# Sorting experts by token count, and six more weight slots, in a two-layer hybrid trunk with a mixture of experts

## The chip, the cores and the metric

The kernel runs on one core of one Trainium2 chip. The metric is the device time of one execution in microseconds; of several runs the median is given.

## The reference

A trunk of two layers runs over 256 tokens at once: 128 context tokens and 128 latent tokens, each of 1024 values. A layer modulates and normalises the tokens, projects them, runs three branches (differential attention, a long convolution, a retention), merges them and adds the result. Then comes a grouped mixture of experts (MoE), the part that the change touches. All arithmetic is in float32.

```python
def moe(h, w_router, b_router, w1, w3, w2):
    scores = jax.nn.softmax((h @ w_router).astype(jnp.float32), axis=-1)
    sel = scores + b_router.astype(jnp.float32)
    grp = sel.reshape(sel.shape[:-1] + (N_GROUPS, EXP_PER_GROUP))
    gscore = lax.top_k(grp, TOP_K)[0].sum(-1)
    gidx = jnp.argmax(gscore, axis=-1)
    ...
    _, eidx = lax.top_k(masked, TOP_K)
    ...
    a = jnp.einsum('bld,edf->blef', h, w1)
    b = jnp.einsum('bld,edf->blef', h, w3)
    act = jax.nn.silu(a) * b * gate[..., None].astype(h.dtype)
    return jnp.einsum('blef,efd->bld', act, w2)
```

There are 16 experts, each token goes to two of them, and an expert has w1 and w3 of 1024x512 and w2 of 512x1024. So 512 places are taken in a layer, 32 for an expert on average.

## The kernel before, in words

**The stream of weights.** All weights are cut into pieces of 128x2048 float32 (1.05 MB). `PLAN` lists every group of pieces in the order in which SyncE's queue fetches them; `ring_table` gives each piece its slot in `ring`, which has 8 slots. Piece n is fetched once n - 7 pieces have been consumed (`s_weights_used`). A dense unit (an input projection, an output projection, half a merge branch) takes one piece, a modulation (`ada`) four, and the MoE of a layer 102. TensorE consumes the pieces in the same order. The MoE fetch is line 534, that of the single item lines 526 and 539, that of dense pieces line 512.

**The MoE.** After the output projection (line 922) the router picks two experts for each token; a modulation `ada(layer, 5)` (line 637) and small matmuls lie between. An expert's tokens are then numbered, and `picks` on VectorE builds a matrix of zeros and ones that gathers them. Eight items follow of two experts each, `PAIRS` of them, with 64 places for an expert. An item p on TensorE is: `moe_in` (line 1014), four blocks, in each of which two experts' matmuls stream 256 columns through two tiles of 64 stationary columns side by side; `gather` of item p + 1 (lines 987 and 997); `act_turn` (line 1039), which transposes the activations; `moe_out` of item p - 1 (line 1050), two halves of 512 columns; and `combine` (line 1092), which adds the scaled result to every token in PSUM banks 0 to 3. ScalarE and VectorE copy and activate between these steps.

A ninth item, the single, has one expert of at most 64 further places, chosen on chip: the first block by which an expert passes 64 places. Its weights are fetched once more. If there are more such blocks, each engine branches to `more_block`, which fetches and computes them one after the other. The single's matmuls are lines 1029, 1069 and 1079.

In layer 0 the items 4 to 7 also carry the filter of the next layer (`filter_step`).

**Other queues.** GpSimd's queue loads parameters and the caches `kc`, `vc` and `sc` of the next layer (line 573 on), exchanges halves for the rotary, stores the new cache entries (lines 587 and 590), and broadcasts rows for the router. The branch buffers (`qk`, `mix`, `kc`, `vc`, `sc`, `filt`, `ysp`, `attr`, `qx`, `xi`, `probs`, `amix`, `amixT`) are tensors of their own, and nothing uses most of them during the MoE.

Of the kernel before, what the change touches and what calls it, by code (L numbers as in the profile page):

```python
# [38 lines left out]
PAIRS = N_EXPERTS // 2  # L39
BLOCK = 64  # L40

MORE = 2 * TOK // (BLOCK + 1) - 1
OVER = (TOK - 1) // BLOCK
# [8 lines left out]
SLOTS = 8  # L52

# [7 lines left out]
ITEMS = PAIRS + 1  # L61
MOE_PIECES = 6 * N_EXPERTS + 6
# [45 lines left out]
def ring_table():  # L108

    pieces = [(item, c) for item in PLAN for c in range(PLAN_PIECES[item[0]])]  # L110
    done = [(item, c) for item in DONE for c in range(PLAN_PIECES[item[0]])]
    slot, count, filled = [], [], [0] * SLOTS
    for n, piece in enumerate(pieces):
# [4 lines left out]
    return slot, count  # L118

SLOT, FILL = ring_table()
# [23 lines left out]
def ff_end(layer, p):  # L145

    before = END["moe", layer, 0] - MOE_PIECES
    return before + 8 * min(p + 1, PAIRS) + 4 * (p // PAIRS) + 4 * max(p - 1, 0)

def y_end(layer, p, half):
# [3 lines left out]
    return ff_end(layer, p + 1) + 2 * (half + 1)  # L155
# [92 lines left out]
def trunk_program(nc, row_scratch, weights, experts, mod_params, params, consts, shared, x_in, k_cache, v_cache, s_cache,  # L248
                  y_out, k_out, v_out, s_out):
    with ExitStack() as ctx:  # L250
# [20 lines left out]
        s_extra_known = sem("extra_known")  # L271
# [92 lines left out]
        s_weights_in = [sem(f"weights_in{slot}") for slot in range(SLOTS)]  # L364
# [20 lines left out]

        ring = sb("ring", P, SLOTS, PIECE)
        cst = sb("cst", P, N_CST)
# [6 lines left out]
        qk = sb("qk", P, 8, TOK)  # L394
        mix = sb("mix", P, 8, TOK)
# [4 lines left out]
        kc = sb("kc", P, H_A, SEQ)  # L400
        vc = sb("vc", P, H_A * DV_A)
        sc = sb("sc", P, H_C, 2, DV_C)
        filt = sb("filt", P, 3, C_B)
        zt = sb("zt", P, C_B)
        ysp = sb("ysp", P, 2, C_B)
        tmp = sb("tmp", P, C_B)
        attr = sb("attr", P, H_C, SEQ)
        qx = sb("qx", P, 2, 2, SEQ)
        dsum = sb("dsum", P, H_C, SEQ)
        xi = sb("xi", P, 2, 2, SEQ)  # L410
        probs = sb("probs", P, 2, 2, 2 * SEQ)
        amix = sb("amix", P, 2, 2 * SEQ)
        amixT = sb("amixT", P, 2, 2 * SEQ)
# [15 lines left out]
        ints = ctx.enter_context(nc.sbuf_tensor("ints", [P, 3], mybir.dt.int32))  # L429
# [3 lines left out]
        xsel = sb("xsel", P, 8)  # L433
# [15 lines left out]
        rows_sb = amixT[0:16, 0, 0:P]  # L449
# [53 lines left out]
        def _(sp):  # L503
            sp.dma_start(x[:, :, :], x_in).then_inc(s_x_in, 16)
            sp.dma_start(shd[:, :], shared).then_inc(s_shared_in, 16)
            n = dense = 0
            for kind, layer, _ in PLAN:
                for _ in range(0 if kind == "moe" else PLAN_PIECES[kind]):
                    if n >= SLOTS:

                        sp.wait_ge(s_weights_used, n - SLOTS + 1)
                    sp.dma_start(ring[:, SLOT[n], :], weights[dense, :, :]).then_inc(
                        s_weights_in[SLOT[n]], 16)
                    n += 1
                    dense += 1
                if kind != "moe":
                    continue
                for p in range(PAIRS + 1):
                    todo = [(2 * p + c % 2, c // 2) for c in range(8)] if p < PAIRS else []
                    if p == PAIRS:  # L520

                        sp.wait_ge(s_extra_known, layer + 1)
                        e = sp.value_load(ints[0:1, 2:3], min_val=0, max_val=N_EXPERTS - 1)
                        for part in (0, 2, 1, 3):
                            sp.wait_ge(s_weights_used, n - SLOTS + 1)
                            sp.dma_start(ring[:, SLOT[n], :], experts[layer, bass.ds(e, 1), part, :, :]
                                         .rearrange("a p c -> (a p) c")).then_inc(
                                             s_weights_in[SLOT[n]], 16)
                            n += 1
                    todo += [(2 * p - 2 + c % 2, 4 + c // 2) for c in range(4)] if p else []  # L530
                    for e_, part in todo:

                        sp.wait_ge(s_weights_used, n - SLOTS + 1)
                        sp.dma_start(ring[:, SLOT[n], :], experts[layer, e_, part]).then_inc(
                            s_weights_in[SLOT[n]], 16)
                        n += 1
                for part in (4, 5):
                    sp.wait_ge(s_weights_used, n - SLOTS + 1)
                    sp.dma_start(ring[:, SLOT[n], :], experts[layer, bass.ds(e, 1), part, :, :]
                                 .rearrange("a p c -> (a p) c")).then_inc(s_weights_in[SLOT[n]], 16)  # L540
                    n += 1
# [7 lines left out]
        def _(pool):  # L549
# [15 lines left out]
            for layer in range(DEPTH):  # L565
# [38 lines left out]
        def _(pe):  # L604
# [10 lines left out]
            def piece(width):  # L615
# [4 lines left out]
                return ring[:, SLOT[n], :].rearrange("p (k n) -> p k n", n=width)  # L620
# [381 lines left out]
            def moe_in(layer, p):  # L1002
# [3 lines left out]
                pe.wait_ge(s_hgat_hi, ITEMS * layer + p + 1)  # L1006
                for half in range(2):
# [1366 lines left out]
```

## Time and profile before

| what | value |
|---|---|
| median of 3 runs (lowest to highest) | 1264.77 us (1264.11 to 1270.05) |
| the profiled execution, its span | 1267.2 us |
| TensorE matmuls, busy | 1228.1 us (97%) |
| TensorE weight loads, busy | 929.2 us (73%) |
| VectorE, ScalarE, busy | 363.3 and 222.0 us |
| bytes moved | 362.06 MB, mean 286 GB/s |
| fetches of expert pieces | 204, of 1024 KB |
| fetches of dense pieces | 128, of 1024 KB |

The profiled execution is one of its own, beside the three timed runs. Its time is the span, from the first to the last instruction. A busy TensorE is one that has a matmul in its pipeline, not one at its peak. In the trace a float32 matmul stands as two instructions, each of which streams all its columns.

### The profile page before, as it was taken

What the parts mean: (1) busy time and instruction counts of PE and PEld (TensorE: products, weight loads), DVE (VectorE), ACT (ScalarE), POOL (GpSimd) and SP (SyncE); (2) the same over time, 40 slices, a digit from 0 to 9 for tenths busy, and PEclk for the clock granted to TensorE, in tenths of its full rate; (3) what the DMA queues carried; (4) which work ended last, traced back from release to release, by engine and by line L of the source; (5) the groups of instructions that cost most, each with busy time, mean ns of one, the idle gap of its engine ahead of it and who ended that gap; (6) DMA issues with size and microseconds to landing.
All of it is one profiled execution on the core that took longest, in us unless ns stands there. A gap on an engine that the chain in (4) does not pass through costs nothing.

```text
span 1267.2 us, 18560 instructions
## 1 busy us (share of the span) xinstructions
PE 1228.1 (97%) x7762; PEld 929.2 (73%) x7762; DVE 363.3 (29%) x917; ACT 222.0 (18%) x469; POOL 39.5 (3%) x80
## 2 busy tenths in 40 slices
PE   6999999999999999999999999999999999999996
PEld 5678888888897666666558888887888776666663
DVE  2441153134236111111233223423243611111113
ACT  2141013231030100111124101223202010000011
POOL 1001110000000000000000012000000000000000
PEclk9899999999989999999999999999999999999999
DMA  9779443424967999999976844343345599999992
GB/s 387 315 290 388 140 158 127 147 100 151 350 254 313 417 421 421 420 420 420 418 293 253 361 161 143 129 141 134 122 149 195 236 418 421 421 420 420 420 421 111
DMA packets 52601, 362.06 MB, mean 286 GB/s; under 512 B 6592, under 2 KB 6752, under 8 KB 9760
## 3 DMA queue, kind: packets, MB, share of 16 engines
q1 hardware_dynamic: 48672, 350.33, 69.3%
q0 software_dynamic: 3840, 10.47, 2.4%
q8 instruction: 64, 1.05, 0.3%
q14 instruction: 25, 0.20, 0.0%
HBM read 356.56 MB, written 2.64 MB: 283 GB/s over the span
## 4 chain that ended last, share of the span: by engine, by line
PE 86%; DMA 9%; DVE 2%; ACT 1%; issue 1%; SPq 0%; DVEq 0%; ACTq 0%
PE bank L713 24%; PE bank L1014 13%; PE bank L1050 9%; DMA ring<-in_experts 7%; PE bank L893 7%; PE bank L997 5%; PE bank L922 4%; PE bank L708 4%; PE bank L637 4%; PE bank L1092 3%; DMA ring<-in_weights 2%; PE bank L724 2%; PE bank L1029 1%; PE bank L973 1%; PE bank L697 1%
## 5 line engine op out<-in xcount | busy, mean ns | idle before, releaser
L713 PE MATMUL bank<-h,ring 128*128 128x256 f32 x1472 | 326.3, 380 | 0.0
L713 PEld LDWEIGHTS bank<-h,ring 128*128 128x128 f32 x1472 | 276.8, 190 | 40.9 <-issue 4.4
L1014 PE MATMUL bank<-ring,gates 128*64 128x256 f32 x2048 | 226.2, 380 | 8.0 <-DMA ring<-in_experts 4.3
L1014 PEld LDWEIGHTS bank<-ring,gates 128*64 128x64 f32 x2048 | 152.1, 137 | 79.7 <-issue 11.6
L1050 PE MATMUL bank<-ring,gates 128*64 128x512 f32 x512 | 113.4, 595 | 0.0
L1050 PEld LDWEIGHTS bank<-ring,gates 128*64 128x64 f32 x512 | 35.3, 137 | 66.7 <-issue 66.7
L997 PE MATMUL bank<-uc,gates 128*128 128x128 f32 x576 | 67.9, 276 | 0.1
L997 PEld LDWEIGHTS bank<-uc,gates 128*128 128x128 f32 x576 | 65.9, 192 | 0.7 <-DVE uc L1612 0.4
L1616 DVE SCALAR_TENSOR_TENSOR gates<-gates,bank 128x512 f32<-128x512 f32 (+1 forms) x18 | 11.8, 658 | 172.6 <-issue 161.3
L1092 PEld LDWEIGHTS bank<-gates,uc 128*128 128x128 f32 x256 | 47.3, 190 | 18.8 <-issue 13.0
L1092 PE MATMUL bank<-gates,uc 128*128 128x256 f32 x256 | 59.5, 386 | 0.0
L708 PE MATMUL bank<-ring,h 128*128 128x256 f32 x256 | 56.4, 379 | 0.0
L922 PE MATMUL bank<-uc,ring 128*128 128x256 f32 x256 | 55.6, 379 | 0.0
L922 PEld LDWEIGHTS bank<-uc,ring 128*128 128x128 f32 x256 | 48.6, 190 | 6.6
L708 PEld LDWEIGHTS bank<-ring,h 128*128 128x128 f32 x256 | 48.1, 190 | 6.2
L1556 ACT ACTIVATE gates<-bank 128x512 f32<-128x512 f32 (+1 forms) x18 | 10.3, 574 | 240.6 <-PE bank L1014 218.7
L637 PE MATMUL bank<-ring,condT 128*32 128x256 f32 x768 | 46.6, 397 | 3.9 <-DMA ring<-in_weights 3.2
L2115 DVE COPY uc<-bank 128x512 f32<-128x512 f32 x16 | 11.1, 692 | 134.9 <-PE bank L1050 134.9
L724 PE MATMUL bank<-h,ring 128*128 128x256 f32 x192 | 43.2, 382 | 2.5 <-ACT h L1268 2.5
L724 PEld LDWEIGHTS bank<-h,ring 128*128 128x128 f32 x192 | 36.0, 190 | 9.4 <-issue 4.6
L637 PEld LDWEIGHTS bank<-ring,condT 128*32 128x32 f32 x768 | 25.8, 114 | 22.5 <-issue 9.7
L1423 ACT ACTIVATE gates<-bank,sm 128x256 f32<-128x256 f32 x48 | 20.1, 471 | 104.9 <-PE bank L713 104.9
(258 smaller groups left out, 1077.6 us busy)
## 6 DMA issues: line engine op xcount, KB each, us to landing
ring<-in_experts SPq DMA_DIRECT2D x204, 1024.0 KB, 11.7
ring<-in_weights SPq DMA_DIRECT2D x128, 1024.0 KB, 6.5
cst<-in_consts POOLq DMA_DIRECT2D x1, 1345.0 KB, 11.2
x<-in_x_in SPq DMA_DIRECT2D x1, 1024.0 KB, 5.0
sc<-in_s_cache POOLq DMA_DIRECT2D x2, 512.0 KB, 10.0
probs<-qk POOLq DMA_DIRECT2D x32, 32.0 KB, 3.0
va<-row_scratch POOLq DMA_DIRECT2D x2, 512.0 KB, 7.2
vr<-row_scratch POOLq DMA_DIRECT2D x2, 512.0 KB, 9.2
```

Source lines behind the costliest of these rows:

```text
L637: last = pe.matmul(bank[b][32 * j:32 * j + 32, 0:256], condT[:, k, :], w[j][:, k, :], start=(k == 0), stop=(k == KT - 1), skip_group_check ...
L697: last = pe.matmul(bank[4][:, 0:TOK], ones[:, :], h[:, k, :], start=(k == 0), stop=(k == KT - 1))
L708: last = pe.matmul(bank[b][:, g * 256:(g + 1) * 256], h[:, k, g_cols(g)], w[:, k, :], start=(k == 0), stop=(k == KT - 1))
L713: last = pe.matmul(bank[b][:, c * TOK:(c + 1) * TOK], w[:, k, c * P:(c + 1) * P], h[:, k, :], start=(k == 0), stop=(k == KT - 1))
L724: last = pe.matmul(bank[u][:, c * TOK:(c + 1) * TOK], w[:, k, c * P:(c + 1) * P], h[:, k, :], start=(k == 0 and c == 0), stop=(k == KT - 1 ...
L893: last = pe.matmul(bank[b][:, c * TOK:(c + 1) * TOK], w[:, k, d * P:(d + 1) * P], src[:, k, :], start=(k == 0), stop=(k == 3))
L922: last = pe.matmul(out[c], w[:, k, c * P:(c + 1) * P], merged[:, k, :], start=(k == 0), stop=(k == KT - 1))
L997: last = pe.matmul(bank[4 + half][:, c * P:(c + 1) * P], htok[:, g, k * P:(k + 1) * P], pick[p % 2][:, g, :], start=(g == 0), stop=(g == 1))
L1014: last = pe.matmul(bank[b][64 * j:64 * j + 64, half * 256:half * 256 + 256], hgat[:, k, 64 * j:64 * j + 64], w[j][:, k, :], start=(k == 0) ...
L1050: last = pe.matmul(bank[5 - half][64 * j:64 * j + 64, :], actT[p % 2][:, f, 64 * j:64 * j + 64], w[j][:, f, :], start=(f == 0), stop=(f == ...
L1092: last = pe.matmul(bank[dt // 2][:, (dt % 2) * TOK:(dt % 2 + 1) * TOK], ysb[:, dt * P:(dt + 1) * P], matrix, start=(fresh and dt % 2 == 0) ...
L1423: last = sc_e.activation(gates[:, t, :], src[:, c, :], ACT.Tanh, scale=0.5, bias=b_half[:, t:t + 1])
```

## The change

The largest and the smallest experts get items of their own kinds. `ITEM_KINDS` replaces the eight pairs and a single with five pairs, a `wide` item (one expert, 128 places), a `quad` item (four experts, 32 places each, in four tiles of 32 columns) and a `single`, which now is one expert fetched once, with its two halves side by side. Experts 12 to 15 are fixed in the first two pairs. Experts 0 to 11 are sorted by their count of tokens on VectorE (`sort`), and fetched by the expert number that the sort leaves in `ints`: the largest is the wide item, the four smallest the quad. No expert is fetched twice, so a layer's MoE takes 96 pieces. `further` counts blocks that don't fit their room; they go to `more_block` as before.

Six further slots are lent to the ring during the MoE. The tensor `lent` has six slots of 2048 columns, in which the branch buffers now lie; only MoE pieces use them, once the last merge piece is consumed and the stores are done. The loads of `kc`, `vc` and `sc` for layer 1 wait for the end of the MoE of layer 0.

```diff
+ITEM_KINDS = ("pair", "pair", "wide", "quad", "pair", "pair", "pair", "single")
+ITEMS = len(ITEM_KINDS)
+PAIRS = ITEMS - 1
+SORTED = 12
+ITEM_EXPERTS = ((12, 13), (14, 15), (0,), (8, 9, 10, 11), (1, 2), (3, 4), (5, 6), (7,))
+FIXED_ITEMS = 2
+WIDE_ROOM, SMALL_ROOM = 128, 32
-MORE = 2 * TOK // (BLOCK + 1) - 1
-OVER = (TOK - 1) // BLOCK
+MORE = 2 * TOK // (BLOCK + 1)
+OVER = (TOK - 1 - SMALL_ROOM) // BLOCK + 1
 SLOTS = 8
+LENT = 6
-MOE_PIECES = 6 * N_EXPERTS + 6
+MOE_PIECES = 6 * N_EXPERTS
...
-        at = n if n < SLOTS else slot[pieces.index(done[n - SLOTS])]
+        lent = range(SLOTS, SLOTS + LENT) if kind == "moe" else ()
+        since = {at: free[at] for at in range(SLOTS)}
+        since.update({at: max(free[at], END["merge", layer, 5]) for at in lent})
+        at = min(since, key=lambda n: (since[n], n))
...
+                sp.wait_ge(s_stores_read, layer + 1)
...
+                for p in range(ITEMS):
+                    if p == FIXED_ITEMS:
+                        sp.wait_ge(s_order_known, layer + 1)
+                    many = len(ITEM_EXPERTS[p])
...
+                    for part in (0, 2, 1, 3) if ITEM_KINDS[p] == "single" else range(4):
+                        for j in range(many):
+                            fetch(expert(p, j, part))
...
+                else:
+                    pool.wait_ge(s_weights_used, END["moe", layer - 1, 0])
                 pool.dma_start(kc[:, :, :], k_cache[layer]).then_inc(s_cache_in, 16)
...
-                        w = piece(256), piece(256)
+                        w = [piece(256) for _ in range(many)]
                         for k in range(KT):
-                            for j in range(2):
-                                last = pe.matmul(bank[b][64 * j:64 * j + 64, half * 256:half * 256 + 256],
-                                                 hgat[:, k, 64 * j:64 * j + 64], w[j][:, k, :],
+                            for j in range(many):
+                                rows = slice(width * j, width * j + width)
+                                last = pe.matmul(bank[b][rows, half * 256:half * 256 + 256],
+                                                 hgat[:, k, rows], w[j][:, k, :],
...
-                    if layer + 1 < DEPTH and p >= 4:
-                        filter_step(layer + 1, p - 4)
+                    if layer + 1 < DEPTH and p >= 3:
+                        filter_step(layer + 1, p - 3)
...
+                def sort():
+                    key, at = place[:, 0, :], place[:, 1, :]
+                    first = C("xf")[:, 0:SORTED]
...
+                    link(stt(key, count[:, 0:SORTED], float(N_EXPERTS), first, ALU.mult, ALU.subtract))
+                    link(tt(square, across(key), down(key), ALU.is_gt))
+                    link(dve.tensor_reduce(at, square, AX.X, ALU.add))
+                    link(stt(places_of[:, :, :], across(at), 1.0, down(first), ALU.add, ALU.is_equal))
+                    link(tt(square, places_of[:, :, :], across(first), ALU.mult))
+                    link(dve.tensor_reduce(key, square, AX.X, ALU.add))
+                    ts(ints[:, 2:2 + SORTED], key, -1.0, ALU.add, 0.0, ALU.max).then_inc(s_order_known, 1)
...
                 gathered(0)
+                sort()
...
                     if p == 0:
-                        block_of(1, ints[:, 2:3], xsel[:, 0:2], xsel[:, 2:4])
-                        dve.sem_inc(s_extra_known, 1)
+                        sort_tokens(sorted_rank, rank)
+                        sort_tokens(sorted_gate, gate)
                         mod_add(layer, 5, 1)
+                        rooms()
+                        further()
```

`sort_tokens` multiplies ranks (or shares) by the matrix of places and adds over experts, two operations of 288 elements; `rooms` writes each expert's room in five; `further` is the former count of blocks (three comparisons, now four after a subtraction, then a running sum in 12 operations), moved from ahead of the first item into it. `picks` builds two operations for each tile and group of tokens, so 4 in the wide item, 8 in a pair and 16 in the quad.

## Rows read from the trace of the kernel before

**Rows 1.** The page: GB/s moved in 40 slices of the span.
```profile
GB/s 387 315 290 388 140 158 127 147 100 151 350 254 313 417 421 421 420 420 420 418 293 253 361 161 143 129 141 134 122 149 195 236 418 421 421 420 420 420 421 111
```
**Rows 2.** The chain of waits, by line, share of the span.
```profile
by line: PE bank L713 24.2%; PE bank L1014 12.8%; PE bank L1050 8.9%; DMA ring<-in_experts 6.8%; PE bank L893 6.6%; PE bank L997 5.2%; PE bank L922 4.4%; PE bank L708 4.4%; PE bank L637 3.6%; PE bank L1092 2.9%; DMA ring<-in_weights 2.5%; P
```
**Rows 3.** Timeline of TensorE, one pair item: start us, us, instructions.
```profile
470.97 14.03 PE L1014 MATMUL bank<-ring,gates 128*64 128x256 f32 x128
...
485.21 3.74 PE L997 MATMUL bank<-uc,gates 128*128 128x128 f32 x32
...
489.31 7.09 PE L1050 MATMUL bank<-ring,gates 128*64 128x512 f32 x32
496.33 3.72 PE L1092 MATMUL bank<-gates,uc 128*128 128x256 f32 x16
499.98 14.25 PE L1014 MATMUL bank<-ring,gates 128*64 128x256 f32 x128
```
**Rows 4.** Timeline of TensorE, input blocks that waited (in brackets) for a fetch.
```profile
540.37 3.67 PE L1014 MATMUL bank<-ring,gates 128*64 128x256 f32 x32 [0.23 <-DMA ring<-in_experts]
...
571.33 3.67 PE L1014 MATMUL bank<-ring,gates 128*64 128x256 f32 x32 [1.29 <-DMA ring<-in_experts]
...
1118.58 3.67 PE L1014 MATMUL bank<-ring,gates 128*64 128x256 f32 x32 [0.36 <-DMA ring<-in_experts]
...
1208.66 3.67 PE L1014 MATMUL bank<-ring,gates 128*64 128x256 f32 x32 [0.62 <-DMA ring<-in_experts]
```
**Rows 5.** Timeline of TensorE, first and last matmuls of the two MoE stages.
```profile
393.15 14.03 PE L1014 MATMUL bank<-ring,gates 128*64 128x256 f32 x128 [0.69 <-ACT gates L1536]
...
645.76 2.94 PE L1079 MATMUL bank<-gates,uc 64*128 64x256 f32 x16 [0.79 <-ACT uc L1547]
...
1000.81 14.03 PE L1014 MATMUL bank<-ring,gates 128*64 128x256 f32 x128 [0.69 <-ACT gates L1536]
...
1250.44 2.94 PE L1079 MATMUL bank<-gates,uc 64*128 64x256 f32 x16 [0.79 <-ACT uc L1547]
```
**Rows 6.** Stretches of time: busy us by engine, PEclk, DMA share, GB/s.
```profile
360.00:365.00 5.00, 5.00 (x25) 4.41 (x24) 1.34 (x5) 0.84 (x3) 0.00 (x0) 1.00 0.36 87
...
380.00:385.00 5.00, 5.00 (x76) 3.39 (x74) 3.93 (x15) 0.00 (x0) 0.00 (x0) 0.93 0.02 7
```
**Rows 7.** Groups by line: busy us, mean ns of one, idle before.
```profile
L713 PE MATMUL bank<-h,ring 128*128 128x256 f32 x1472 | 326.3, 380 | 0.0
...
L1014 PE MATMUL bank<-ring,gates 128*64 128x256 f32 x2048 | 226.2, 380 | 8.0 <-DMA ring<-in_experts 4.3 <-ACT gates L1536 3.7
...
L1050 PE MATMUL bank<-ring,gates 128*64 128x512 f32 x512 | 113.4, 595 | 0.0
...
L637 PE MATMUL bank<-ring,condT 128*32 128x256 f32 x768 | 46.6, 397 | 3.9 <-DMA ring<-in_weights 3.2 <-DVEq L1622 0.7
...
L1608 DVE TENSOR_TENSOR dsum<-dsum,zt 128x256 f32<-128x256 f32 x14 | 5.9, 422 | 1.5
```
**Rows 8.** Issue to landing of line 534's fetches; timeline of GpSimd, stores.
```profile
DMA to landing us min/median/max: 4.7/11.6/16.8
...
207.35 1.08 POOL L590 DMA_DIRECT2D s_out<-mix  x2 [25.97 <-ACT mix L1455]
```
**Rows 9.** TensorE's modulation after a pause, the clock there, and without one.
```profile
40.66 6.35 PE L637 MATMUL bank<-ring,condT 128*32 128x256 f32 x64 [2.91 <-DMA ring<-in_weights]
...
40.00:50.00 10.00, 9.34 (x79) 5.97 (x80) 0.63 (x4) 1.44 (x2) 0.00 (x0) 0.69 0.24 86
...
381.54 3.66 PE L637 MATMUL bank<-ring,condT 128*32 128x256 f32 x64
```
**Rows 10.** Timeline of VectorE, the first MoE item of layer 0.
```profile
398.26 0.21 DVE L1616 SCALAR_TENSOR_TENSOR tmp<-cnt 128x48 f32<-128x48 f32 x1
...
404.40 0.69 DVE L1616 SCALAR_TENSOR_TENSOR gates<-gates,bank 128x512 f32<-128x512 f32 x1 [2.15 <-ACT gates L1556]
```

More of the change, by code:

```diff
@@ L111, in ring_table @@
     done = [(item, c) for item in DONE for c in range(PLAN_PIECES[item[0]])]
-    slot, count, filled = [], [], [0] * SLOTS
-    for n, piece in enumerate(pieces):
-        at = n if n < SLOTS else slot[pieces.index(done[n - SLOTS])]
+    gone = {piece: n + 1 for n, piece in enumerate(done)}
+    free, filled = [0] * (SLOTS + LENT), [0] * (SLOTS + LENT)
+    slot, count, used = [], [], []
+    for (kind, layer, _), c in pieces:
+        lent = range(SLOTS, SLOTS + LENT) if kind == "moe" else ()
+        since = {at: free[at] for at in range(SLOTS)}
+        since.update({at: max(free[at], END["merge", layer, 5]) for at in lent})
+        at = min(since, key=lambda n: (since[n], n))
         filled[at] += 1
@@ L117, in ring_table @@
         count.append(filled[at])
-    return slot, count
-SLOT, FILL = ring_table()
+        used.append(since[at])
+        free[at] = gone[(kind, layer, _), c]
+    return slot, count, used
+SLOT, FILL, USED = ring_table()
 ADA_ORDER = [item[1:] for item in PLAN if item[0] == "ada"]
@@ L147, in ff_end @@
     before = END["moe", layer, 0] - MOE_PIECES
[L148 removed]
+    return before + sum(ITEM_IN[:p + 1]) + sum(ITEM_OUT[:max(p - 1, 0)])
 def y_end(layer, p, half):
@@ L154, in y_end @@
         return END["moe", layer, 0]
-    return ff_end(layer, p + 1) + 2 * (half + 1)
+    return ff_end(layer, p + 1) + ITEM_OUT[p] // 2 * (half + 1)
 def combined(layer, p):
@@ L363, in trunk_program @@
         s_vr_copied = sem("vr_copied")
-        s_weights_in = [sem(f"weights_in{slot}") for slot in range(SLOTS)]
+        s_weights_in = [sem(f"weights_in{slot}") for slot in range(SLOTS + LENT)]
         s_weights_used = sem("weights_used")
@@ L393, in trunk_program, with part @@
         uc = sb("uc", P, 12, TOK)
-        qk = sb("qk", P, 8, TOK)
-        mix = sb("mix", P, 8, TOK)
+        def part(slot, at, n):
+            return lent[:, slot, at:at + n]
+        qk = part(0, 0, 2048).rearrange("p (a b) -> p a b", a=8)
+        mix = part(1, 0, 2048).rearrange("p (a b) -> p a b", a=8)
         qkr = mix[:, 0:4, :]
@@ L506, in _, with fetch @@
             n = dense = 0
-            for kind, layer, _ in PLAN:
[L508 to L515, printed above, removed]
+            def fetch(source):
+                nonlocal n
+                if USED[n]:
+                    sp.wait_ge(s_weights_used, USED[n])
+                slot = ring[:, SLOT[n], :] if SLOT[n] < SLOTS else lent[:, SLOT[n] - SLOTS, :]
+                sp.dma_start(slot, source).then_inc(s_weights_in[SLOT[n]], 16)
+                n += 1
@@ L516, in _ @@
+            for kind, layer, _ in PLAN:
                 if kind != "moe":
+                    for _ in range(PLAN_PIECES[kind]):
+                        fetch(weights[dense, :, :])
+                        dense += 1
                     continue
[L518 to L536, printed above, removed]
@@ L537, in _ @@
                 for part in (4, 5):
[L538 to L541, printed above, removed]
+                    fetch(expert(PAIRS, 0, part))
             for c in range(4):
@@ L2144, in _, with further @@
-                upto = src
-                ts(ints[:, 0:1], upto[:, OVER * N_EXPERTS - 1:], -1.0, ALU.add, 0.0,
-                   ALU.max).then_inc(s_more_known, 1)
+                def further():
+                    nonlocal upto, other
+                    beyond = place[:, :, :].rearrange("p a b -> p (a b)")[:, 0:N_EXPERTS]
+                    link(tt(beyond, count, room[:, :], ALU.subtract))
+                    for c in range(OVER):
+                        link(ts(flags[:, 16 * c:16 * c + 16], beyond, float(BLOCK * c), ALU.is_gt))
+                    src, dst = flags, upto
+                    step = 1
+                    while step < OVER * N_EXPERTS:
+                        link(dve.tensor_copy(dst[:, 0:step], src[:, 0:step]))
+                        link(tt(dst[:, step:], src[:, step:], src[:, :OVER * N_EXPERTS - step], ALU.add))
+                        src, dst = dst, (other if dst is upto else upto)
+                        step *= 2
+                    upto = src
+                    dve.tensor_copy(ints[:, 0:1], upto[:, OVER * N_EXPERTS - 1:]).then_inc(s_more_known, 1)
@@ L2164, in block_of @@
-                    link(ts(red[:, 1:2], red[:, 1:2], -float(BLOCK), ALU.mult))
+                    level = one.rearrange("p (c e) -> p e c", e=N_EXPERTS)
+                    byexp, start, part_ = tmp[:, 64:80], tmp[:, 80:96], tmp[:, 96:112]
+                    link(dve.tensor_reduce(byexp, level, AX.X, ALU.add))
+                    link(tt(part_, byexp, C("xf")[:, 0:16], ALU.mult))
+                    link(dve.tensor_reduce(red[:, 0:1], part_, AX.X, ALU.add))
+                    link(ts(expert, red[:, 0:1], -1.0, ALU.add, 0.0, ALU.max))
@@ L2165, in block_of @@
+                    link(tt(start, byexp, room[:, :], ALU.mult))
+                    for c in range(1, OVER):
+                        link(stt(start, one[:, 16 * c:16 * c + 16], float(BLOCK * c), start, ALU.mult, ALU.add))
+                    link(dve.tensor_reduce(red[:, 1:2], start, AX.X, ALU.add))
+                    link(ts(red[:, 1:2], red[:, 1:2], -1.0, ALU.mult))
                     wide_ = tmp[:, 128:160].rearrange("p (a b) -> p a b", a=2)
```

170 lines of the change are left out of this document (96 added, 74 removed).

## The prediction

> **What bounds the kernel now.** I read the row of bytes moved over the span first [rows 1]: twice, for about eight and about seven slices of 31.7 us, transfers run flat at 420 GB/s, and these are the two mixture-of-experts (MoE) stages. Outside them they run at 120 to 350. The chain of waits [rows 2] puts 6.8% on the expert fetches and most of the rest on TensorE, so neither limit stands alone. The timeline of one pair item [rows 3] shows why: TensorE goes from one item's first matmul (470.97) to the next one's (499.98) in 29.01 us without a pause: input matmuls 14.0, gathers and turns 4.4, output matmuls 7.0, combine 3.65. A pair needs 12 pieces of weights of 1.05 MB. Where TensorE does wait for a fetch in layer 1, the first and last such waits end 90.1 us apart [rows 4] with 36 pieces between: 2.50 us a piece, 30.0 us a pair. So an item costs 29.0 on TensorE and 30.0 on the DMA engines, and the eight-slot lead hides the difference: the six waits of both layers add up to 4.3 us [rows 4, 7], 1.5 of it in layer 0. The MoE stages last 393.15 to 648.70 and 1000.81 to 1253.38 [rows 5], 255.6 and 252.6 us; layer 0 is longer by the filter matmuls of layer 1.
>
> Ahead of a stage the ring is full and the transfers idle: 87 GB/s in 360 to 365, 7 GB/s in 380 to 385 [rows 6]. That is the room that lent slots could fill.
>
> **Part 1: one item fewer.** Before there are eight pairs and a single; after, seven full-length items and a single. I take TensorE's time for each form. The wide item has one expert over all 128 columns: 16 passes of 128x256 per block at 326.3/1472 = 0.222 us, 3.55 us a block as against 14.03/4 = 3.51 for a pair [rows 3, 7]; it fetches 6 pieces. The quad has four 32-column tiles side by side and fetches 24. Four-way tiles of 256 columns are in the trace, in the modulation (line 637): 64 instructions in 3.66 us [rows 9], the size of one quad block, so 3.6 us where a pair takes 3.51. Four-way with 512 columns (quad output) is not in the trace; nearest is line 1050, two-way at 113.4/512 = 0.221 a pass [rows 7]. If four run at once it is 0.11 each, 7.1 us per item as for a pair; if only two at once, 14.2. Line 637 has four at once at 46.6/768 = 0.061, so I take 7.1. Not less, since the same columns stream. The whole item therefore disappears: 29.0 us of TensorE time per layer.
>
> **Part 2: 96 pieces for 102.** The expert with over 64 places was fetched a second time. Six pieces of 2.50 are 15.0 us of transfer per layer.
>
> **Part 3: six lent slots.** Slots 8 to 13 come free when the last merge piece is consumed, before the output projection. There are then 14 pieces in flight or landed when the first item starts, not 8. The idle room of [rows 6] takes the six: the transfers are far from busy in the 25 us before 385. The last four of the 14 wait, as four do now, for the modulation that ends at 385.2 [rows 9]. Six pieces by 2.50 are another 15.0 us of lead per layer. The fetch queue also waits for the stores of the branch outputs; the last is issued at 207.35 [rows 8], over 130 us earlier, so nothing.
>
> **What is then late: the transfers at the quad.** TensorE alone would gain 29.0 + 1.5 and 29.0 + 2.8, but the quad asks for 24 pieces in 29 us and the fetch gives 11.6. I walked the stage piece by piece: a piece lands 2.50 us after the one before it, or, if its slot was released late, 4.7 us after the release (the shortest issue-to-landing of these fetches [rows 8]). Layer 0: pieces 11 to 14 are released at 385.2 and land to 397.4. Every piece up to 43 arrives before TensorE wants it; around the wide item, which frees 6 slots in its 29 us, all 14 are full and the transfers pause 8 us in all. At the quad's first block (471.2) number 40 lands and 32 are wanted; its fourth block wants number 44 at 482.0, just as it lands, a wait of 0.1. Pair 4 is served. The quad's second output half wants number 62 at 523.1 and it lands at 527: a wait of 4.0. Then 0.5 and 1.5 in pair 5's last two blocks, and none after: the last items want fewer pieces than arrive (number 96 at 612, wanted at 617.4). In all 6.1 us: the stage ends at 393.15 + 225.4 + 6.1 = 624.7 as against 648.7, **24.0 less** (225.4 is 255.6 - 1.5 - 29.0, plus 0.4 for the slightly longer quad blocks). Layer 1 lacks the filter matmuls, so the same walk has waits of 4.4, 0.8, 1.5 and 0.9 with the 0.1, 7.7 in all: 252.6 - 2.8 - 29.0 + 0.4 + 7.7 = 228.9 us, **23.7 less**.
>
> **The clock behind such a wait.** A pause of 2.91 us before line 637 at 40.66 is followed by 6.35 us for 64 instructions that take 3.66 elsewhere, and the granted clock of 40 to 50 is 0.69: part of it ran at the lower level of 1.2 GHz [rows 9]. The wait of 4.0 is longer, so I add 2.7 per layer. Half or more is absorbed, since the waits that follow (1.9 in layer 0, 3.2 in layer 1) are for pieces that don't come later for it: 0.8 and 0. The Trainium skill, "TensorE: Matmul & The Clock Gate", HAM oscillation, says that waits for a transfer between bursts of matmuls drop the clock, each time anew; the trace agrees with its one pause. By that rule the sum is as here; without it 0.8 less.
>
> **The small steps.** VectorE's sort (7 operations, at most 144 elements), sorting of ranks and shares (4, of 288), room (5) and two more operations in the count of further blocks come in; the block search (15 operations) goes from the first item. At 0.21 for 48 elements and 0.42 for 256 [rows 7, 10] that is 2.5 + 1.8 + 1.0 + 0.4 - 3.4 = 2.3 us more, ahead of an operation before which VectorE now idles 2.15 [rows 10]. The activation's second operation waits for TensorE as long again. I cost it at 0; above, if every operation cost 0.42, some 4 us more would be late and go to TensorE's turn of the first item, 2 to 4 per layer. Below, no gain: the path was not VectorE's. The order is known near 394, while piece 21, the first that needs it, has its slot released at 407. The fetch queue's reading of an expert number is in the trace too (the single), and an issue costs it 0.34 us per 2.50. Quad picks are 16 operations for 8, some 1.5 us more under 14 us of input matmuls. The caches of layer 1 are loaded after the MoE of layer 0 instead of in its idle room: 1 MB, 2.5 us, in GpSimd's queue, wanted some 17 units of 7.1 us (32 passes of 0.222) later, and the next thing in that queue waits for unit 7 anyhow: 0. Filter steps only move an item forward.
>
> **Sum.** 24.0 + 23.7 - 0.8 = 46.9 us. The profiled execution's span is 1267.2, 2.4 above the median of the runs; off the median 1264.8 it is **1217.9 us**, span about 1220.
>
> **Rivals.**
> *TensorE alone decides (12%).* If pieces land a little earlier than in my walk or TensorE is held elsewhere anyway, the waits vanish: 2 x 29.0 + 4.3 = 62.3, 1202.5 us; with a third of the waits 1207. For it: the measured waits are as small as 0.2. Against: 24 pieces in 29 us cannot come from the stream.
> *The lent slots bring little (12%).* If their fetches start late or crowd out other transfers, each missing slot costs 2.50 per layer, first at the quad's input; all six: 30.0, so 1248. Half: 1233. Against: the idle rows.
> *Quad tiles overlap only in pairs (6%).* Input and output of the quad each double, 21 us per layer, of which about 8 hide in the waits: 1244. Line 637 speaks against it for the input.
> *An expert does not fit its room (slower, 3%).* The wide item serves only the largest of experts 0 to 11, and 12 to 15 keep 64 places. No instruction of the further-block branch is in the trace, so now at most one expert per layer passes 64, once. Routing the reference's own inputs gives expert 2, with 85 and 91; next come 43 and 50, and the fourth smallest of the first twelve has 27 and 15 for 32 places. If instead an expert of 12 to 15 passed 64, or the fourth smallest 32, a serial block runs: six fetches through two buffers, about 4.1 us each ((3.55 + 4.7)/2), gather, activations and combine, some 40 us. In both layers that is 1218 + 80 = 1298; it decides against the change from two such blocks.
> *My forecast (64%)* spans 1208 to 1230; the remaining 3% is for outcomes that none of these names, two thirds of it no change.
>
> **How the numbers follow.** The range takes the forecast's own, three quarters of the first rival and two thirds of the second: 1204 to 1240. About 0.5% (6 us) is what a measurement of this kernel can tell. Slower is the last rival, 0.03; within 0.5%, 0.02; the rest faster, 0.95.
>
> **What would show it.** MoE stages of 231 and 229 us; 96 expert fetches per layer, 192 in all; no or one short gap in transfers until the quad; TensorE's longest wait for a fetch, 4 us, before the second half of the quad's output, followed by slowed matmuls; quad blocks of 3.6 us. Wrong if the quad's blocks take 7 us, if large waits stand in the quad's input (a lead that did not form), or if rows of the further-block branch appear.

## The result

The changed kernel took 1218.28 us (median of 4 runs, 1217.30 to 1220.16) where the kernel before took 1265.04 (4 runs): a ratio of 0.962, 95% interval 0.959 to 0.965, 46.8 us less. The forecast was 1217.9. The profiled execution was the slowest of the four: its span is 1218.4 and its own time 1220.16, so 1.8 us lie around the span.

The page of the changed kernel, its rates in 40 slices, answers to [rows 1]. A slice is now 30.5 us.

```profile
PEclk8999999999998999999999999999999899999998
DMA  9879534333797998999986945343247599899992
GB/s 383 339 284 393 183 130 142 136 112 139 278 408 306 405 401 341 421 421 420 421 331 258 373 153 165 113 147 138 107 155 314 231 391 416 326 423 420 421 420 109
```

Two things are to be seen. The idle room ahead of the MoE is used: the two slices that end near 366 us carry 278 and 408 where two slices at about that place carried 350 and 254, and the same 5 us that moved 87 GB/s before [rows 6] now move 423:

```profile
360.00:365.00 5.00, 5.00 (x25) 4.40 (x24) 1.98 (x6) 2.00 (x6) 0.00 (x0) 1.00 1.01 423
380.00:385.00 5.00, 4.50 (x74) 2.86 (x66) 2.23 (x6) 0.38 (x1) 0.00 (x0) 1.00 0.12 16
```

From 380 to 385 the transfers are idle as before: all slots that are free are filled. And there is a dip inside each stage (341, 326) that the kernel before did not have: the ring is full there, around the wide item.

The issues of transfers on the same page, with KB each and the median from issue to landing:

```profile
ring<-in_weights SPq DMA_DIRECT2D x128, 1024.0 KB, 5.7
ring<-in_experts SPq DMA_DIRECT2D x108, 1024.0 KB, 20.9
lent<-in_experts SPq DMA_DIRECT2D x84, 1024.0 KB, 16.7
```

108 and 84 are 192 expert pieces, where there were 204. They are under way for 17 to 21 us instead of 12, because more are queued.

The timeline of TensorE in layer 0 (start, length, instructions, in brackets the idle time before) from the first to the last matmuls of the stage answers to [rows 3 to 5]:

```profile
391.40 10.58 PE L1056 MATMUL bank<-lent,gates 128*64 128x256 f32 x96 [0.69 <-ACT gates L1580]
...
440.12 13.98 PE L1056 MATMUL bank<-ring,gates 128*128 128x256 f32 x64
...
468.92 3.86 PE L1056 MATMUL bank<-lent,gates 128*32 128x256 f32 x66
...
480.86 0.41 PE L1056 MATMUL bank<-ring,gates 128*32 128x256 f32 x2 [1.37 <-DMA lent<-in_experts]
...
488.74 7.03 PE L1095 MATMUL bank<-lent,gates 128*128 128x512 f32 x16
...
517.86 0.62 PE L1095 MATMUL bank<-ring,gates 128*32 128x512 f32 x2
...
526.36 5.13 PE L1095 MATMUL bank<-lent,gates 128*32 128x512 f32 x32 [4.86 <-DMA lent<-in_experts]
531.42 3.72 PE L1136 MATMUL bank<-gates,uc 128*128 128x256 f32 x16
...
620.60 2.94 PE L1123 MATMUL bank<-gates,uc 64*128 64x256 f32 x16 [0.79 <-ACT uc L1591]
```

The stage lasts 391.40 to 623.54, 232.1 us (before 255.6), and in layer 1, by the same rows, 975.29 to 1204.58, 229.3 us (before 252.6). The two stages together are 46.7 us shorter, which is all that the medians differ by. The first half of the quad's output starts at 517.86; its matmuls run until 521.5, then comes the longest wait of the stage. The granted clock of the 10 us around that wait is 0.83 (third number from the end):

```profile
520.00:530.00 10.00, 5.14 (x36) 1.29 (x32) 0.00 (x0) 1.88 (x2) 0.00 (x0) 0.83 1.01 420
```

TensorE's waits over the whole changed kernel (sum, times, longest):

```profile
PE bank L1095 <- DMA lent<-in_experts: 9.5, 2, 4.9
...
PE bank L1056 <- ACT gates L1580: 3.7, 4, 1.2
...
PE bank L1056 <- DMA lent<-in_experts: 3.5, 2, 2.1
...
PE bank L1056 <- DMA ring<-in_experts: 1.3, 3, 0.6
```

14.3 us of waits for expert fetches, where there were 4.3: the change adds waits, and still gains, because the item that went was worth more.

### The profile page after: what moved, and what is told of

The parts are those of the page before. It is cut to its first block, busy times and chain, and to the rows that moved or that the text cites. A ratio compares the mean times of both kernels' runs of the same rounds, so it can differ in the third digit from the quotient of the medians.

```text
span 1218.4 us, 18282 instructions
## 1 busy us (share of the span) xinstructions
PE 1171.0 (96%) x7494; PEld 897.5 (74%) x7494; DVE 359.9 (30%) x905; ACT 216.3 (18%) x459; POOL 39.5 (3%) x80
## 3 DMA queue, kind: packets, MB, share of 16 engines
q8 instruction: 62, 1.02, 0.3%
## 4 chain that ended last, share of the span: by engine, by line
PE 87%; DMA 8%; DVE 2%; ACT 1%; SPq 1%; issue 1%; DVEq 0%; ACTq 0%
PE bank L752 25%; PE bank L1056 12%; PE bank L1095 7%; PE bank L932 7%; PE bank L961 5%; PE bank L747 5%; PE bank L1036 4%; DMA ring<-in_experts 4%; PE bank L763 4%; PE bank L1136 4%; PE bank L676 4%; DMA lent<-in_experts 3%; DMA ring<-in_weights 1%; PE bank L1071 1%; PE bank L1012 1%; SPq L541 1%
## 5 line engine op out<-in xcount | busy, mean ns | idle before, releaser
L752 PEld LDWEIGHTS bank<-h,ring 128*128 128x128 f32 x1472 | 276.8, 190 | 40.9 <-issue 4.4
L1056 PE MATMUL bank<-ring,gates 128*64 128x256 f32 (+2 forms) x1280 | 148.7, 379 | 7.1 <-DMA lent<-in_experts 3.5
L1056 PEld LDWEIGHTS bank<-ring,gates 128*64 128x64 f32 (+2 forms) x1280 | 104.3, 137 | 45.4 <-issue 7.5
L1095 PE MATMUL bank<-lent,gates 128*64 128x512 f32 (+2 forms) x288 | 67.0, 637 | 9.5 <-DMA lent<-in_experts 9.5
L1056 PE MATMUL bank<-lent,gates 128*64 128x256 f32 (+1 forms) x640 | 64.7, 380 | 1.4 <-ACT gates L1580 1.4
L932 PE MATMUL bank<-lent,ring 128*128 128x256 f32 x256 | 56.4, 380 | 0.0
L1056 PEld LDWEIGHTS bank<-lent,gates 128*64 128x64 f32 (+1 forms) x640 | 39.2, 126 | 21.2 <-issue 2.3
L1095 PEld LDWEIGHTS bank<-lent,gates 128*64 128x64 f32 (+2 forms) x288 | 21.3, 141 | 44.9 <-issue 44.9
L932 PEld LDWEIGHTS bank<-lent,ring 128*128 128x128 f32 x256 | 48.4, 190 | 6.9 <-issue 0.4
L1136 PE MATMUL bank<-gates,uc 128*128 128x256 f32 x224 | 51.9, 385 | 0.0
```

The lines of the kernel that those rows point to most:

```text
L752: last = pe.matmul(bank[b][:, c * TOK:(c + 1) * TOK], w[:, k, c * P:(c + 1) * P], h[:, k, :], start=(k == 0), stop=(k == KT - 1))
L932: last = pe.matmul(bank[b][:, c * TOK:(c + 1) * TOK], w[:, k, d * P:(d + 1) * P], src[:, k, :], start=(k == 0), stop=(k == 3))
L1056: last = pe.matmul(bank[b][rows, half * 256:half * 256 + 256], hgat[:, k, rows], w[j][:, k, :], start=(k == 0), stop=(k == KT - 1), skip_g ...
L1095: last = pe.matmul(bank[5 - half][rows, :], actT[p % 2][:, f, rows], w[j][:, f, :], start=(f == 0), stop=(f == 3), skip_group_check=True)
L1136: last = pe.matmul(bank[dt // 2][:, (dt % 2) * TOK:(dt % 2 + 1) * TOK], ysb[:, dt * P:(dt + 1) * P], matrix, start=(fresh and dt % 2 == 0) ...
```

## The experiments

Each ran beside the kernel before on its chip; those of one group shared the chip and its runs. The length of a MoE stage is read from the timeline of the profiled execution as above. What lies outside the two stages took between 752.8 and 759.1 us in these profiled executions, whatever the variant, so a difference of a few us between two medians need not come from the MoE; the stages are the better measure. The profile of one_block is taken apart in its own paragraph.

| run | time, us | ratio to before, 95% interval | stages, layer 0 and 1, us |
|---|---|---|---|
| changed kernel | 1218.28 | 0.962 (0.959 to 0.965) | 232.1, 229.3 |
| no_lent | 1254.53 | 0.989 (0.986 to 0.992) | 251.5, 247.8 |
| lent_alone | 1258.32 | 0.993 (0.990 to 0.995) | 253.3, 248.9 |
| quad_first | 1215.58 | 0.957 (0.952 to 0.961) | 230.8, 226.8 |
| half_fetch | 1209.43 | 0.954 (0.951 to 0.957) | 233.2, 219.3 |
| after_again | 1217.22 | 0.961 (0.959 to 0.963) | 232.3, 229.7 |
| busy_wait | 1219.80 | 0.963 (0.961 to 0.964) | 232.2, 229.7 |
| quad_late | 1217.13 | 0.962 (0.960 to 0.964) | 231.7, 228.9 |
| quad_first_busy | 1210.05 | 0.955 (0.953 to 0.956) | 229.0, 225.3 |
| sort_four | 1219.26 | 0.963 (0.960 to 0.965) | 233.2, 229.8 |
| one_block | 1266.57 (one run) | | |

**no_lent: the new items, eight slots.**

```diff
-        lent = range(SLOTS, SLOTS + LENT) if kind == "moe" else ()
+        lent = ()
```

> The new items with a ring of 8 slots; nothing is lent. By the walk of the prediction the transfers are six pieces behind at the quad: six times 2.50 us in each layer, stages of 232 + 15 and 229 + 15 us, 1218 + 30 = 1248 us, with TensorE's waits in the quad's input blocks (about 1, 7 and 6 us). Rival: the lead is not what counts, since 96 pieces of 2.50 us fit into a stage anyway; then within 5 us of 1218.

1254.5, so the rival falls: the lead does count, and the six slots are worth 36 us beside the new items (38 by the stages). That is 6 more than walked. The quad's input blocks on the timeline of this run:

```profile
470.71 3.66 PE L1056 MATMUL bank<-ring,gates 128*32 128x256 f32 x64
476.35 5.35 PE L1056 MATMUL bank<-ring,gates 128*32 128x256 f32 x64 [1.98 <-DMA ring<-in_experts]
488.42 6.15 PE L1056 MATMUL bank<-ring,gates 128*32 128x256 f32 x64 [6.72 <-DMA ring<-in_experts]
498.34 6.31 PE L1056 MATMUL bank<-ring,gates 128*32 128x256 f32 x64 [3.77 <-DMA ring<-in_experts]
```

The waits are where the walk put them (2.0, 6.7, 3.8 for 1, 7, 6), and the quad's output waits 5.6 more. The blocks behind the three take 5.4 to 6.3 us instead of 3.7. Set against the changed kernel, layer 0 has 11.7 us more of waits, less than the walked 15, and 7.6 us of slower matmuls and restarts. The walk had no clock in it, and the clock is what was missing:

```profile
480.00:490.00 10.00, 3.28 (x48) 1.82 (x44) 0.00 (x0) 0.00 (x0) 0.00 (x0) 0.83 1.00 419
490.00:500.00 10.00, 6.23 (x68) 3.10 (x64) 0.69 (x1) 0.60 (x1) 0.00 (x0) 0.67 1.00 400
```

Granted clock (third from the end) 0.83 and 0.67, transfers busy all the time.

**lent_alone: the old items, fourteen slots.**

```diff
--- (the kernel before)
-        at = n if n < SLOTS else slot[pieces.index(done[n - SLOTS])]
+        lent = range(SLOTS, SLOTS + LENT) if kind == "moe" else ()
+        ...
+        at = min(since, key=lambda n: (since[n], n))
```

with the branch buffers moved into `lent` as in the change.

> The items of the kernel before (eight pairs, a single, 102 pieces) with the six lent slots. By the walk TensorE is then the only limit: the 4.3 us of waits go, 1265 - 4 = 1261 us. Rival: the lead is worth 15 us per layer by itself, as it is at the quad: 1235 us.

1258.3, 8.8 us under the kernel before on that chip. No wait for an expert fetch is left, and the stages are 2.3 and 3.6 us shorter, 5.9 in all: the 4.3 of waits and the 0.2 to 0.3 that each of the six had cost beyond its own length (in layer 0 an item with a wait of 0.23 took 29.82 us and takes 29.37 here). The rest lies outside the stages, where executions vary. The lead alone is worth little: TensorE has its 29 us an item.

The two parts by themselves gain 12.6 and 8.8 us, 21 together (8.9 and 5.9 in the stages); both at once gain 46.8 to 49.7 (46.7 in the stages). Fewer items without a lead run into the transfers, a lead without fewer items runs into TensorE.

**half_fetch: TensorE without a limit by transfers, in layer 1.** Part of the weights is missing from layer 1's MoE.

```diff
+                if half:
+                    slot, source = slot[:, 0:PIECE // 2], source[:, 0:PIECE // 2]
                 sp.dma_start(slot, source).then_inc(s_weights_in[SLOT[n]], 16)
...
-                            fetch(expert(p, j, part))
+                            fetch(expert(p, j, part), layer == 1)
```

> The changed kernel, but in layer 1 each expert piece is fetched only in its first half of columns, so that part of the weights is missing from layer 1's MoE. Transfers can't limit that stage. If the waits for fetches are the only thing between TensorE's own 221 us and the measured 229.3, the stage takes 221.2 us (252.6 - 2.8 - 29.0 + 0.4) and the kernel 1218 - 8 = 1210 us. Rival: other waits (copies, VectorE's longer first item) hold part of it: 224 us or more.

The stage of layer 1, which lasts until 1191.50:

```profile
972.25 10.58 PE L1058 MATMUL bank<-lent,gates 128*64 128x256 f32 x96 [0.69 <-ACT gates L1582]
...
1188.57 2.94 PE L1125 MATMUL bank<-gates,uc 64*128 64x256 f32 x16 [0.79 <-ACT uc L1593]
```

It takes 219.3 us: 10.0 less than in the changed kernel, 1.9 under the 221.2 walked. So neither copies nor VectorE hold the stage beyond the walk, as the rival had it, and the whole distance between TensorE's own time and the measured stage is 7.9 us of waits and 2.1 of slower matmuls and restarts behind them.

The 1.9 below the walk can be taken apart on the timelines. The waits of the kernel before had cost 0.9 more than their length, the 0.4 for slower quad blocks does not exist (a quad block takes 3.5 us, like a pair's), and the items around the wide one and the quad go 0.7 faster (28.92, 28.80 and 28.65 us from first matmul to first matmul, where a pair between pairs takes 29.01). Set against lent_alone, which has the old items and no waits either, the new items save 29.7 us in layer 1 (248.9 to 219.3), where 29.0 was forecast.

**quad_first: the quad third, the wide fourth.**

```diff
-ITEM_KINDS = ("pair", "pair", "wide", "quad", "pair", "pair", "pair", "single")
+ITEM_KINDS = ("pair", "pair", "quad", "wide", "pair", "pair", "pair", "single")
```

(and the experts' places in `ITEM_EXPERTS` likewise)

> The changed kernel with the quad as third item and the wide one as fourth. The walk gives waits of 1.1 (quad's input) and 0.2 and 1.5 in the item after next, none in the quad's output, since the wide item, which takes 6 pieces, follows at once: 3.7 us less in layer 0 and 4.9 in layer 1, and the 1.5 us of slowed matmuls behind the long wait go too, partly. 1218 - 9 = 1209 us, between 1207 and 1211. Rival: the order doesn't matter because the bytes are the same: 1218 us.

1215.6, with runs of 1207.9, 1214.0, 1217.1 and 1217.4: neither the forecast nor clearly the rival. The interval of its ratio (0.952 to 0.961) overlaps that of the changed kernel (0.959 to 0.965); the stages are 1.3 and 2.5 us shorter. In the profiled execution, the one of 1217.1, the wait in the quad's input was 4.95 us, not 1.1, and the block behind it ran at half the clock:

```profile
456.40 0.64 PE L1056 MATMUL bank<-lent,gates 128*32 128x256 f32 x2 [4.95 <-DMA ring<-in_experts]
```

```profile
450.00:455.00 5.00, 1.45 (x28) 0.62 (x20) 0.69 (x1) 0.60 (x1) 0.00 (x0) 0.88 1.02 423
455.00:460.00 5.00, 3.60 (x36) 2.02 (x40) 0.00 (x0) 0.00 (x0) 0.00 (x0) 0.50 1.01 421
```

The transfers never stopped (423 and 421 GB/s), so piece 36 came 3.9 us later than walked with the bytes on time. The last section says what was seen of it.

**quad_late: the quad sixth, the wide seventh.**

```diff
-ITEM_KINDS = ("pair", "pair", "wide", "quad", "pair", "pair", "pair", "single")
+ITEM_KINDS = ("pair", "pair", "pair", "pair", "pair", "quad", "wide", "single")
```

(and the experts' places likewise)

> The changed kernel with the quad as sixth and the wide as seventh item. The walk gives one wait, 3.8 us in the quad's input, and stages 3.0 and 3.9 us shorter than in the walk of the changed kernel; the late landings seen with the quad as third item (3.5 us later than walked) take some of it back, and a pause costs clock: between 1209 and 1216, 1212 us. Rival: the order doesn't matter beyond the noise: 1218 us.

1217.1 against 1217.2 of the unaltered kernel: no gain, just above the expected bound. The walk's one wait of 3.8 is 6.2 us in layer 0 and 6.6 in layer 1, with a slow block behind:

```profile
542.06 0.64 PE L1056 MATMUL bank<-ring,gates 128*32 128x256 f32 x2 [6.22 <-DMA lent<-in_experts]
```

The stages are 231.7 and 228.9 us where the walk gives 228.5 and 225.0.

**after_again and busy_wait: the clock behind the long wait.**

> The changed kernel unaltered, as the base for its variants on the same chip: 1218 us, between 1216 and 1221.

```diff
                 for half in range(2):
+                    if many == 4 and half:
+                        take(5 - half)
+                        for _ in range(18):
+                            pe.matmul(bank[5 - half][:, 0:P], ones[:, :], ones[:, :], start=True, stop=True)
...
                     w = [piece(512) for _ in range(many)]
```

> The changed kernel with 18 dummy matmuls (about 4.5 us, a third of whose time at most can stick out) issued ahead of the wait for the second half of the quad's output. If the matmuls behind the wait are slow (5.1 us for 3.6) because TensorE paused, they take 3.6 us now, and in layer 1, and less in layer 0, up to 1.5 us is gained: 1216.5 us, a difference near what can be measured; the trace row decides. Rival: they are slow because of the interleaved fetches or tiles: then still 5.1 us, and 1218 us or more.

The trace shows the mechanism without its gain:

```profile
518.77 4.29 PE L1093 MATMUL bank<-ones 128*128 128x128 f32 x36
...
523.61 3.64 PE L1100 MATMUL bank<-lent,gates 128*32 128x512 f32 x32 [0.55 <-DMA lent<-in_experts]
...
543.47 3.67 PE L1056 MATMUL bank<-ring,gates 128*64 128x256 f32 x32 [1.29 <-DMA ring<-in_experts]
```

The half behind the wait takes 3.64 us and not 5.13, so it was the pause. But the next item's fourth block now waits 1.29 for its fetch (0.16 in the changed kernel), and the stages are 232.2 and 229.7, as in the kernel without dummies (232.3 and 229.7 in after_again). The transfers set the pace until that block, and a slow TensorE costs nothing while they do. The median is no better either: 0.963 (0.961 to 0.964) against 0.961 (0.959 to 0.963).

**quad_first_busy: dummies in the order of quad_first.**

```diff
--- (quad_first)
+                        if many == 4 and (half, b) == (1, 7):
+                            for _ in range(12):
+                                pe.matmul(bank[7][:, 256:256 + P], ones[:, :], ones[:, :], start=True,
+                                          stop=True, skip_group_check=True)
                         w = [piece(256) for _ in range(many)]
```

> Quad as third item, with 12 dummy matmuls (about 3 us) ahead of the wait for the fourth block of its input. The four runs of that order without them spread from 1207.9 (granted clock 0.993) to 1217.4 us (0.984). If the spread is the clock behind the 5 us wait, it closes here near the fast end: 1209 to 1211 us with a clock of 0.99. Rival: the spread has another cause (transfers that land late by chance), the dummies change nothing: 1215 us, same spread.

1210.05 us, all five runs within 1208.9 to 1210.9, clock 0.992 to 0.994. That is 7.2 us under the changed kernel on the same chip (0.955, 0.953 to 0.956, against 0.961, 0.959 to 0.963), the best version found. Order and dummies together gain this; what the dummies give by themselves is less clear, since quad_first has 0.957 (0.952 to 0.961), which overlaps.

The traces tell more. The dummies took 2.95 us and left a wait of 0.24 in layer 0 and 1.02 in layer 1, and the fourth block runs at full clock. So the quad item is 3.9 and 3.4 us shorter than in quad_first (32.2 and 33.0 us for 36.1 and 36.4). Two items later a wait for a fetch appears that quad_first did not have:

```profile
512.82 3.67 PE L1060 MATMUL bank<-lent,gates 128*64 128x256 f32 x32 [1.31 <-DMA lent<-in_experts]
```

That item is 1.9 and 2.0 us longer, and the stages are 1.8 and 1.5 us shorter in all (229.0 and 225.3 for 230.8 and 226.8). About half of what the dummies save at the quad thus comes back as a later wait. The profiled executions differ by 6.6 us, and 3.3 of it lies outside the stages, where nothing was changed. That the spread closed is as expected, but the cause of the spread isn't shown: the kernel before has no such wait and spreads from 1264.6 to 1270.9 on the chip of quad_first.

**sort_four: VectorE's cover.**

```diff
+                    if again:
+                        return
                     ts(ints[:, 2:2 + SORTED], key, -1.0, ALU.add, 0.0, ALU.max).then_inc(s_order_known, 1)
...
                 sort()
+                again = True
+                dve.wait_ge(s_order_known, layer + 1)
+                for _ in range(3):
+                    sort(again)
```

> The changed kernel with the six chained steps of the sort done three times more in each layer (unused), about 3 x 1.9 = 5.7 us of VectorE's time ahead of the first item's activation. By the prediction's account the cover is used up (2.3 us added into an idle of 2.15, as long again behind it), so some 3.5 us per layer go to TensorE: 1225 us. Rival: the turn of the first item waits for the next gather anyway and the item after it for ScalarE, so that about 3 us more are hidden: under 1 us per layer, 1218 to 1220 us.

1219.3, stages 1.1 and 0.5 us longer: the rival. Counted from the start of the stage, VectorE's picks for the second item end 5.9 us later, and of that TensorE sees this:

```profile
411.05 0.66 PE L1081 MATMUL bank<-cst,gates 128*128 128x128 f32 x4 [0.42 <-DVE gates L1652]
412.59 10.58 PE L1056 MATMUL bank<-ring,gates 128*64 128x256 f32 x96 [0.89 <-DVE gates L2184]
```

0.42 at the turn, and 0.89 where the changed kernel waits 1.17 for ScalarE anyhow: the first item is 0.4 us longer (20.16 for 19.80), in layer 1 too. The other 0.7 of layer 0 is a longer wait for a fetch in the quad's input, 2.37 us for 1.37, which nothing here ties to VectorE.

**one_block: the price of an expert that does not fit.** Layer 1's result counts some tokens twice.

```diff
-                    link(ts(extra, at, 0.0, ALU.is_equal, float(WIDE_ROOM - BLOCK), ALU.mult))
+                    link(ts(extra, at, 0.0, ALU.is_equal, 0.0 if layer else float(WIDE_ROOM - BLOCK), ALU.mult))
```

> The changed kernel with the wide item's room counted as 64 in layer 1 alone, so that the further-block branch runs once there, on tokens already served (layer 1's result counts them twice). The prediction's price of a block is 40 us: 1258 us. A block under 24 us would mean that an expert that does not fit costs less than the change gains even if one does so in each layer; over 47, that one is enough.

1266.6 us in its one run, 48 more than the changed kernel and 49 more than after_again on its chip. By the traces, from the start of layer 1's stage to the end of the span, it takes 294.8 us where the changed kernel takes 243.1: about 52 us for the block. The chain on TensorE:

```profile
1205.23 0.66 PE L1152 MATMUL bank<-cst,uc 128*128 128x128 f32 x2 [5.81 <-DVEq L2304]
1205.68 5.54 PE L1155 MATMUL bank<-uc,gates 128*128 128x128 f32 x32
1213.25 7.17 PE L1164 MATMUL bank<-lent,gates 128*128 128x256 f32 x32 [2.02 <-DVEq L2309]
1221.96 7.20 PE L1164 MATMUL bank<-lent,gates 128*128 128x256 f32 x32 [1.53 <-DMA lent<-in_experts]
```

It begins with 5.8 us in which VectorE looks for the block, and the gather behind that takes 5.54 where it takes 3.74 in an item: the granted clock from 1203 to 1209 is 0.50.

## Why the prediction was right

**One item fewer, 29.0 us a layer: right.** The wide item's input blocks take 13.98 us for the walked 14.2, and four tiles of 32 columns do stream at once, also with 512 columns (7.1 us walked; 3.6 a half in the trace), the one price that no row of before had. half_fetch beside lent_alone measures the new items at 29.7 us in layer 1.

**96 pieces, and the lead of six slots: right in kind.** The two are not terms that add up: they decide when TensorE's floor can be reached. no_lent and lent_alone show it for the lead. No run has the new items with 102 pieces, so what the six pieces fewer are worth by themselves is not shown. The walk undersized the lead (30 us for 36), since it had no clock in the waits that a missing lead brings.

**What is late then: right in the main place, near in size.** Forecast for layer 0 were waits of 0.1, 4.0, 0.5 and 1.5, measured 1.4, 4.9, 0.2 and none; for layer 1, 7.7 in all, measured 2.1, 4.6, 0.6 and 0.6, 7.9 in all. The wait in the quad's input was undersized, 0.1 for 1.4 and 2.1, and the waits in pair 5's last blocks were oversized. The stages were forecast at 231.5 and 228.9 and took 232.1 and 229.3. That these agree to 0.6 us is in part luck. In layer 1 TensorE's own time was walked at 221.2 and is 219.3 (half_fetch), 1.9 too long, and the walked stage left out the 2.1 us of slow matmuls and restarts behind the waits; the two errors cancel.

**The clock.** Forecast 2.7 us slower behind the long wait, measured 1.5 (5.13 for 3.64), and forecast absorbed all but 0.8 by later waits; busy_wait shows it absorbed entirely. After every wait of 3.8 us or more in the MoE stages of these runs (3.8 to 8.4) the granted clock fell, each time anew: 0.83 in 520 to 530 of the changed kernel, 0.50 in 455 to 460 of quad_first; with dummies in the wait it did not. The Trainium skill, "TensorE: Matmul & The Clock Gate", HAM oscillation, says that waits for a transfer between bursts of matmuls drop the clock each time; the traces agree. What it costs is decided by what sets the pace behind it: nothing in busy_wait, 1.5 to 1.8 us a layer in the quad-first order, by one profiled execution of each kernel.

**The small steps at nothing: right, with too little cover claimed.** The prediction feared 2 to 4 us a layer from 4 us more on VectorE; 5.9 cost 0.4 at the first item. It had counted the idle time before VectorE's two activation steps and missed that the turn comes after the gather.

**The rivals.** "The lent slots bring little" was refuted; so were quad tiles that overlap in pairs. "TensorE alone decides" was refuted by the 14.3 us of waits. The rival on the other side did not occur, no further block ran, but its price was undersized, 48 to 52 us for 40. So the point from which it decides is one such block, not two: one expert over its room takes the whole gain of 47 to 50 us. This was measured once and in layer 1 alone; the price in layer 0 is not known. Unlike the kernel before, the changed one has that risk for experts 12 to 15, which keep 64 places, and for the fourth smallest.

**Outside the stages** the two profiled executions differ by 2.1 us. In that of before a wait at the start of 2.9 us was followed by a slow modulation [rows 9], in that of the changed kernel there is one of 2.0, and the modulation's matmuls near 41 take 3.66. That varies from execution to execution (the first stage starts at 391.4 us in this one and at 393.1 in after_again, the same kernel; over all variants between 387.4 and 393.2) and is no part of the change.

## What to carry to other kernels

Where an engine and the transfers are within a few per cent of each other, remove from both at once: either alone gained 9 and 13 us here, both together 47. Walk the stream piece by piece against the consumer, with the landing time of a piece and the release of its slot; it says where the lead runs out. Trust it for the place more than for the size: it gave the stages within 1 us in the order of the change, partly by errors that cancel, and was 3 to 4 us a stage too short in the two other orders. Where the lead runs out, look at what sets the pace behind the wait: keep the matmul engine busy with dummies only where that is the engine itself, and expect a part of the gain to come back as a later wait.

## What the runs showed of the hardware

```
kernel before, layer 0      spread us     step us
  piece landing at 540.3    2.35          2.48
  piece landing at 543.9    3.49          3.63
  the next twenty           3.5           2.5
quad_first, layer 0
  landing at 388.9, 391.4   0.45, 0.50    - , 2.53
  landing at 395.3, 397.8   1.90, 1.86    3.88, 2.45
  landing at 419.4          1.94          2.46
  landing at 426.4          3.70          3.98
  until 466                 3.65          2.5
```

After a pause of all transfers the sixteen parts land within 0.4 to 0.8 us of each other. Now and then a step is 1.1 to 1.6 us longer than the others and the spread grows by as much, and in these stretches it didn't shrink again while the queue had fetches waiting: every later piece is late by as much, while the rate stays at 420 GB/s. In quad_late the spread ahead of its long waits is 3.2 and 3.6 us. By its size this accounts for most of the 3.9 us by which quad_first missed its walk, and for the wait of 1.29 us beside one of 0.23 in the kernel before [rows 4]. In the changed kernel the full ring at the wide item lets the transfers pause, and the spread falls from 3.7 to 0.7 us just ahead of the quad (3.9 to 0.5 in layer 1); that fits with its walk holding where those of other orders did not. What holds a part up was not tried, and neither was a run that removes it.
